# Reading the moving operands of the two MLP matrix products from the last token to the first

## The reference, cut to what matters

```python
def trunk_layer(x, ...):
    h = rms_norm(x, g_mix)
    ...
    x = x + jnp.concatenate([oa, ob, oc, od], axis=-1) @ w_out
    x = x + jnp.square(jax.nn.relu(rms_norm(x, g_mlp) @ w_up)) @ w_down
    x = x + (ple.astype(x.dtype) @ w_ple) * jax.nn.sigmoid(rms_norm(x, g_ple) @ w_ple_gate)
```

## Time and profile before

| what | value |
|---|---|
| time, median of 3 runs | 3421.33 us (3421.15 to 3425.25) |
| span of the profiled execution | 3410.4 us |
| instructions in the span | 60576 |
| PE busy | 3303.6 us, 97% of the span |
| POOL busy | 2257.7 us, 66% |
| DVE busy | 1241.0 us, 36% |
| ACT busy | 1161.5 us, 34% |
| mean granted TensorE clock | 0.988 of full speed |

### The profile page before, as it was taken

One profiled execution on the slowest core, in us unless ns is written; L12 is line 12 of the kernel. 1 busy time (PEld: TensorE's weight loads), 2 busy tenths in 40 slices (PEclk: granted clock), 3 DMA queues, 4 the chain that ended last, 5 costly groups with the idle time before them and its releaser, 6 DMA issues.

```text
span 3410.4 us, 60576 instructions
## 1 busy us (share of the span) xinstructions
PE 3303.6 (97%) x20676; PEld 2990.1 (88%) x20676; DVE 1241.0 (36%) x2237; ACT 1161.5 (34%) x1686; POOL 2257.7 (66%) x2989
## 2 busy tenths in 40 slices
PE   7999999999999999999989999999999999999998
PEld 5776766799999999999977776668999999999998
DVE  4334564543051230423253445645412403204143
ACT  3333332433333333334343432424333233333342
POOL 5664200498898888888765551006988988889885
PEclk9999999999999999999999999999999999999999
DMA  5443422345555555554454433223555554555543
GB/s 157 127 124 107 119 69 84 104 142 154 150 150 153 147 149 155 145 152 142 142 152 115 131 93 105 75 81 118 150 154 149 149 155 144 153 150 152 150 142 124
DMA packets 295726, 453.09 MB, mean 133 GB/s; under 512 B 36336, under 2 KB 111344, under 8 KB 294832
## 3 DMA queue, kind: packets, MB, share of 16 engines
q1 hardware_dynamic: 295328, 448.66, 45.0%
q0 software_dynamic: 144, 0.87, 0.1%
HBM read 435.54 MB, written 14.06 MB: 132 GB/s over the span
## 4 chain that ended last, share of the span: by engine, by line
PE 89%; issue 3%; DVE 3%; ACT 2%; DMA 1%; POOL 1%; SPq 0%; DVEq 0%; POOLq 0%; ACTq 0%
PE ps L706 20%; PE ps L707 20%; PE ps L705 20%; PE ps L803 5%; PE ps L791 5%; PE ps L766 5%; PE ps L769 4%; PE ps L768 3%; PE ps L895 2%; DMA ring<-in_w_in 1%; PE ps L930 1%; PE ps L899 1%; PE ps L841 1%; PE ps L898 1%; POOL wlo L668 1%
## 5 line engine op out<-in xcount | busy, mean ns | idle before, releaser
L668 POOL TENSOR_TENSOR wlo<-ring,whi 128x256 fp32r<-128x256 f32 x2400 | 1831.1, 796 | 789.8 <-ACT whi L1142 789.8
L1142 ACT ACTIVATE whi<-ring 128x1024 fp32r<-128x1024 f32 x600 | 636.0, 1061 | 1339.4 <-PE ps L707 1324.4
L705 PE MATMUL ps<-xhi,wlo 128*128 128x320 f32 x2560 | 791.0, 309 | 13.9 <-POOL wlo L668 10.2
L706 PE MATMUL ps<-xlo,whi 128*128 128x320 f32 x2560 | 795.3, 311 | 0.0
L707 PE MATMUL ps<-xhi,whi 128*128 128x320 f32 x2560 | 791.5, 309 | 0.0
L707 PE MATMUL ps<-hhi,whi 128*128 128x320 f32 x2176 | 672.2, 309 | 0.0
L705 PE MATMUL ps<-hhi,wlo 128*128 128x320 f32 x2176 | 659.3, 303 | 0.1
L654 POOL TENSOR_TENSOR rlo<-ring,whi 128x256 fp32r<-128x256 f32 (+2 forms) x576 | 423.0, 767 | 319.0 <-ACT whi L1126 318.9
L706 PE MATMUL ps<-hlo,whi 128*128 128x320 f32 x2048 | 629.8, 308 | 0.0
L705 PEld LDWEIGHTS ps<-xhi,wlo 128*128 128x128 f32 x2560 | 485.2, 190 | 17.1 <-issue 15.3
L706 PEld LDWEIGHTS ps<-xlo,whi 128*128 128x128 f32 x2560 | 483.0, 189 | 0.8
(11 more groups left out here) (246 smaller groups left out, 3116.0 us busy)
## 6 DMA issues: line engine op xcount, KB each, us to landing
ring<-in_w_up SPq DMA_DIRECT2D x256, 512.0 KB, 3.7
ring<-in_w_down SPq DMA_DIRECT2D x256, 512.0 KB, 3.8
ring<-in_w_in SPq DMA_DIRECT2D x120, 512.0 KB, 3.6
ring<-in_w_out SPq DMA_DIRECT2D x64, 512.0 KB, 3.9
ring<-in_w_ple_gate SPq DMA_DIRECT2D x64, 512.0 KB, 3.8
xsave<-x SPq DMA_DIRECT2D x8, 640.0 KB, 5.7
x<-xsave SPq DMA_DIRECT2D x8, 640.0 KB, 4.5
ring<-in_w_in SPq DMA_DIRECT2D x16, 288.0 KB, 2.9
```

Of the source, the lines that this page charges most:

```text
L668: last = nc.gpsimd.tensor_tensor(wlo[:, s, c:c + LO_COLS], ring[:, s, c:c + LO_COLS], whi[:, s, c:c + LO_COLS].bitcast(f32), ALU.subtract)
L705: mm(out, lo[:, k, cols], xh, start=start, stop=False)
L706: mm(out, hi[:, k, cols], xl, start=False, stop=False)
L1142: A(whi[:, s, :], ring[:, s, :], ACT.Copy).then_inc(hi_ready, 1)
```

## The change

`w_up` gets `x_block_turned` and `w_down` gets `hid_block_turned`: the same blocks, their 320 columns named from the last to the first. The result of `w_up` therefore stands in PSUM with the tokens reversed, so DVE reads the per-token factor `rfeat` in reverse as well, and `hhi` and `hlo` are stored with the tokens reversed. `w_down` reads them in reverse again, so that its result has the tokens in the order of `x`. Outputs in PSUM, the stationary operands, all counts, waits and the order of instructions stay as they are; no instruction is added or removed. The gate product and the tail of `w_out` go on reading forwards, with `x_block` and `last_block`.

```diff
             def x_block(k):
                 return xhi[:, k, :], xlo[:, k, :]

+            def x_block_turned(k):
+                return xhi[:, k, ::-1], xlo[:, k, ::-1]
+
             def last_block(k):
                 return hhi[:, OUT_K[1][1] + k, :], hlast[:, k, :]

-            def hid_block(k):
-                return hhi[:, k, :], hlo[:, k, :]
+            def hid_block_turned(k):
+                return hhi[:, k, ::-1], hlo[:, k, ::-1]
...
-                        gemm_chunk(l, Q_MLP + 16 * g + 2 * c, c % 2, 4 + 8 * g + c, x_block,
+                        gemm_chunk(l, Q_MLP + 16 * g + 2 * c, c % 2, 4 + 8 * g + c, x_block_turned,
...
-                        gemm_chunk(l, Q_MLP + 8 + 16 * g + 2 * c, c % 2, 8 + 8 * g + c, hid_block,
+                        gemm_chunk(l, Q_MLP + 8 + 16 * g + 2 * c, c % 2, 8 + 8 * g + c, hid_block_turned,
...
                             ins = V.scalar_tensor_tensor(out=t0[:, m % 2, :], in0=ps[:, 4 * (c % 2) + m, 0:TOK], scalar=0.0,
-                                                         in1=rfeat[:, :], op0=ALU.max, op1=ALU.mult)
+                                                         in1=rfeat[:, ::-1], op0=ALU.max, op1=ALU.mult)
```

## The result

The change costs about 0.3%. In runs taken side by side, the median went from 3421.15 us (3417.56 to 3425.25, 5 runs) to 3430.03 us (3424.15 to 3436.29, 5 runs); the recorded ratio is 1.0033, with a 95% interval of 1.0016 to 1.0049 (the two medians alone give 1.0026). The profiled execution's span grew from 3410.4 to 3423.3 us.

The account below looks back on a forecast made before the run. The prediction took PE's streaming of the moving operand in the MLP matmuls as the bound. It summed 3410.4 us of span, 10.9 us around it, 0 for matmuls and 0 for DVE to 3421.3 us, range 3414 to 3559.

Parts of the forecast that it names:

- The bound: MLP: PE's matmul pace, set by streaming the moving operand, bounds the kernel; one ns on each of 12288 matmuls is 12.3 us.
- The 10.9 us around the span: Whole kernel: time added outside the profiled span of 3410.4 us to reach the forecast.
- VectorE: L1776: 128 instructions reading `rfeat` backwards cost 0, at most +544 ns each, 70 us in all, covered by PE.
- between these ends I take 0 ns: MLP matmuls: backward read costs nothing, chosen between a gain of 11.2 ns and a loss of 128.0 ns each.
- 12288 x 0: `w_up` and `w_down`: 12288 backward matmuls, 0 ns added on each.
- 0.56 ns per matmul: Turned MLP matmuls: a larger change of pace would prove the forecast wrong; 6.8 us spread over them.
- (b): Seam between two MLP matmuls: each backward start costs up to 11.2 ns more, +137 us, 3559 us; chance 0.10.
- the likeliest case: Whole kernel: backward reading changes nothing, 3421 us, own range 3414 to 3428; chance 0.70 including operands not read backwards.
- 2.9 to 3.1: MLP: sign of the seam rival, the us that the starts of 20 turned matmuls would span, against 2.89.
- (a): MLP matmuls: backward streams run at half rate, 272.5 for 144.5 ns, +1573 us, 4994 us; chance 0.16.
- rows 4 and 5: Profile rows of `w_up` and `w_down`: 20 forward matmuls start over 2.89 us, 144.5 ns each, the basis for zero cost.
- the control: Gate product: 512 forward matmuls whose starts would not spread if reading backwards has a price in the MLP.

Follow-up runs that it names:

- down_only: The changed kernel with the reversal undone in `w_up`, so only `w_down` reads backwards; 3426.67 against 3413.61 us for the kernel before, ratio 1.0035.
- lo_back: The kernel before with only `hlo` stored turned and read backwards in `w_down`; 3422.24 us against 3419.18 us, one run.
- fwd_pad0: The kernel before, all forwards, with `xlo` 64 bytes earlier, 0 modulo 128 from `xhi`; 3416.40 us beside 3413.61 us, one run.
- back_n256: The changed kernel with backward `w_down` on 256 of 320 columns, part of its work left out; 3259.17 us beside a before of 3419.18 us.
- words_back: The changed kernel with groups of four columns read forwards and the four inside backwards; 3414.69 us against 3411.89 us before, one run.
- fwd_pad192: The kernel before, all forwards, with `xlo` padded 192 instead of 64 bytes behind `xhi`; 3407.58 against 3411.12 us, ratio 0.9984.

## Why the prediction was right or wrong

**The bound: right.** The MLP goes at PE's pace and every nanosecond of a matmul reaches the end: 2.2 ns on each `w_down` matmul were 13.7 us of trace, and `down_only` is 1.0035.

**The 10.9 us around the span: misread, without effect.** In every run with a span on record the time is 1.8 to 1.9 us above it (3425.11 and 3423.3 us for the changed kernel). By that the profiled execution of the kernel before took some 3412 us, an estimate, and the other 9 us are its distance from the median. The sum came out at the median all the same. But the two spans, 12.9 us apart, are single executions; the medians are 8.9 us apart.

**VectorE: right.** Its backward reads cost 0 (481 ns against 482), of SBUF and of PSUM. By the Trainium skill, Vector Engine (DVE) Microarchitecture Reference, section 5.2, a port streams at the full rate only while its elements come in runs of two or more adjacent words that start on an 8-byte boundary. Whether words read in descending order count as such a run is not said there; here they lost nothing.

**The matmuls: wrong, and by size.** The step that failed is "between these ends I take 0 ns". The sum's term 12288 x 0 measured 6144 x 2.2 ns = 13.7 us in `w_down` and 6144 x some 0.36 ns = 2.2 us in `w_up`, 15.9 us where I had 0. I had written that 0.56 ns per matmul would decide, and on average it is 1.3. The measured 3430.03 us lies inside the stated range, but that range was wide for the sake of (b); the likeliest case was no change, with 3414 to 3428, and slower had 0.26.

**Which rival it was.** (b), the seam, with 2.2 ns or less in place of the 11.2 I priced. It had a chance of 0.10. Twenty turned matmuls at 146.7 ns take 2.93 us, inside the 2.9 to 3.1 written down for it. Its mechanism was named rightly as far as the runs go: the loss is gone at 256 columns and in `lo_back` stands ahead of the turned stream, so it is not a slower rate of the columns. Its cause was not, since a seam of that length is no property of beginning at the end: `fwd_pad0` has it forwards and `back_n256` lacks it backwards. (a), the half rate, is out by far: 2.2 ns, not 128, and in `words_back` descending words cost nothing.

**The reason behind the zero.** "The nearest rows are those of the same instruction, rows 4 and 5" took 2.89 us for 20 as the pace of that instruction. The trace of before contradicts this in three places that I did not read. Forward `w_up` itself has two paces, 83.65 and 85.27 us for 576, shown above; that rows 4 lie in one of the three fast groups of eight is chance. The gate's forward products, named as the control, have the two paces as well: 28.30 us for a chunk in both layers before, 28.30 and 27.73 us in the changed kernel, so that a shift of 3 ns there proves nothing. And the small product with `w_ple`, 320 columns and forwards, goes at (1585.10 - 1581.14) us / 27 = 146.7 ns, the very pace of the changed kernel:

```profile
1581.14 0.31 PE L706 MATMUL ps<-plel,whi 128*128 128x320 f32 x1
...
1585.10 0.31 PE L706 MATMUL ps<-plel,whi 128*128 128x320 f32 x1
```

144.4 was thus not the cost of such a matmul but the low end of what it takes, for operands that happen to lie so. With 146.7 ns as the ordinary seam the sum would have been +2.2 ns on `w_down` and about nothing on `w_up`: 13.7 us, 3435 us.

**Left open.** What at the seam sets the 13.3, 16 or more periods. The runs show that forwards it hangs on where the moving operands and the weights lie and on the pace fallen into before; that backwards it was the same for every layout at 320 columns, and different at 256 and 304. Why the turned stream loses the 140.0 ns step from L705 to L706 is not shown. That two read streams meet in the memory would fit, but was only argued. The order in which the weights are read was not changed in any run.

## What to carry to other kernels

Where back-to-back matmuls are the bound, read their pace over whole stages and in every stage that runs the same shape before calling it a constant: here the same instruction goes at 144.4, 146.7 or 147.4 ns, and 3 ns on 12288 matmuls are 37 us, more than this change cost. Reading an operand backwards cost VectorE nothing, and TensorE nothing at 256 columns and 2.2 ns of 144.4 at 320, where the layout had gained at the seams; so a change of order, of padding or of column count should be tried together with the others. Where a change of 0.3% comes from is told by the stage lengths in two traces, which agree to some 0.05 us where the pace is the same, sooner than by run times that scatter by 0.2 to 0.6% themselves.

## What the runs showed of the hardware that was not expected

The seam between two matmuls comes in steps: 40 and 48 periods of 1.2 GHz for three matmuls in most stages, others beside them. Forwards, one stretch of code can hold either of two paces for a whole stage (83.65 or 85.27 us for 576 matmuls) and in `fwd_pad192` hands it on to the next (84.86 then 112.64 us, 83.66 then 110.93 us). The forward first chunk of the next `w_up`, 192 matmuls right behind `w_down`, shows the same: it takes 27.74 us behind a forward `w_down` in the kernel before, 935.25 - 907.51, and 28.30 us behind a backward one in `down_only`, 940.84 - 912.54. The end of this chunk before:

```profile
935.25 0.70 PE L749 MATMUL ps<-acc,ones 128*128 128x320 f32 x2
```

and in `down_only`:

```profile
940.84 0.70 PE L749 MATMUL ps<-acc,ones 128*128 128x320 f32 x2
```

Behind these two matmuls of the normalisation `w_up` goes on at either pace. Which one it is differs from group to group within one execution; that it makes part of the scatter between runs of the kernel before would fit, but no second trace of one kernel was taken. Backwards no second pace was seen at 320 columns.
